# The reversed read of the exponential bias table: from GpSimd's DMA queue to SP's, behind the store it reads

## The reference, cut to what matters

```python
rel = kloc[None, :] - qloc[:, None]                          # (BLOCK, 3*BLOCK)
bias = rel_bias[t5_bucket(rel)].astype(jnp.float32)          # (BLOCK, 3*BLOCK, H)
valid = (jnp.abs(rel) <= WINDOW)[None] & (kpos >= 0) & (kpos < S)
s = jnp.einsum('bnqhgd,bnkhd->bnhgqk', qb, kb) * scale + bias
s = jnp.where(valid[None, :, None, None], s, NEG_INF)
p = jax.nn.softmax(jnp.concatenate([s, sink_col], axis=-1), axis=-1)[..., :-1]
o = jnp.einsum('bnhgqk,bnkhd->bnqhgd', p.astype(v.dtype), vb)
```

## Time and profile before

| | |
|---|---|
| median of 3 runs | 972.08 us (971.94 to 972.39) |
| the profiled execution's own time | 972.42 us |
| its span, slowest core (core 3) | 971.4 us |
| spans of the eight cores | 966.9 to 971.4 us |
| PE busy | 937.4 us, 97% of the span |
| DVE, ACT, POOL busy | 65%, 45%, 27% |
| granted TensorE clock, mean | 0.994 on core 3 |

### The profile page before, as it was taken

One profiled execution on the slowest core, in us unless ns is written; L12 is line 12 of the kernel. 1 busy time (PEld: TensorE's weight loads), 2 busy tenths in 40 slices (PEclk: granted clock), 3 DMA queues, 4 the chain that ended last, 5 costly groups with the idle time before them and its releaser, 6 DMA issues.

```text
span 971.4 us, 16466 instructions; the slowest of 8 cores (966.9 to 971.4 us)
## 1 busy us (share of the span) xinstructions
PE 937.4 (97%) x5501; PEld 437.3 (45%) x5501; DVE 631.5 (65%) x1049; ACT 437.5 (45%) x720; POOL 260.2 (27%) x281
## 2 busy tenths in 40 slices
PE   3999999999999999999999999999999999999996
PEld 1454544553445444444445444444444444444442
DVE  1313476665777757565669798886565666664887
ACT  1125657575663444444457456655110444443111
POOL 3200000111135335343333245543200133333002
PEclk9999999998999999999999999999999999999999
DMA  9998134482439999710668176675533323220312
GB/s 132 163 176 160 24 76 102 64 151 51 66 65 127 119 142 129 103 65 2 131 205 337 31 158 170 165 175 129 173 130 112 111 90 114 85 93 7 131 65 87
DMA packets 39683, 112.12 MB, mean 115 GB/s; under 512 B 4976, under 2 KB 16888, under 8 KB 38608
## 3 DMA queue, kind: packets, MB, share of 16 engines
q0 software_dynamic: 11104, 41.16, 29.2%
q1 hardware_dynamic: 28496, 69.91, 22.7%
HBM read 132.49 MB, written 30.47 MB: 168 GB/s over the span
## 4 chain that ended last, share of the span: by engine, by line
PE 88%; DMA 4%; ACT 3%; DVE 2%; issue 2%; POOL 0%; DVEq 0%; ACTq 0%; POOLq 0%; SPq 0%
PE ps L238 87%; DMA arena<-w_q 2%; DMA arena<-xt 1%; ACT arena L604 1%; DMA gexp_scratch<-arena 1%; PE ps L1283 1%; ACT arena L652 1%; DVE arena L597 0%; ACT arena L607 0%; PE ps L767 0%; PE ps L695 0%; POOL arena L152 0%; ACT arena L731 0%; ACT arena L1521 0%; DVE arena L826 0%
## 5 line engine op out<-in xcount | busy, mean ns | idle before, releaser
L238 PE MATMUL ps<-arena 128*128 128x512 bf16 (+5 forms) x5091 | 921.2, 359 | 23.3 <-DMA arena<-xt 14.6
L238 PEld LDWEIGHTS ps<-arena 128*128 128x128 bf16 (+2 forms) x5091 | 417.2, 98 | 510.1 <-issue 66.8
L1332 ACT COPY arena<-ps 128x512 f32<-128x512 f32 x132 | 76.5, 587 | 132.0 <-PE ps L238 132.0
L1342 POOL TENSOR_TENSOR arena<-arena 128x512 bf16<-128x512 f32 x66 | 89.6, 1358 | 142.0 <-DVE arena L1335 141.9
L1335 DVE TENSOR_TENSOR arena<-arena,ps 128x512 f32<-128x512 f32 x132 | 88.0, 684 | 39.8 <-PE ps L238 39.6
L947 POOL TENSOR_TENSOR arena<-arena 128x512 f32<-128x512 f32 (+1 forms) x48 | 63.8, 1337 | 104.3 <-DVE arena L938 104.1
L1198 ACT ACTIVATE arena<-arena 128x1024 bf16<-128x1024 f32 x26 | 27.5, 1058 | 93.6 <-DVE arena L1647 87.5
L938 DVE SCALAR_TENSOR_TENSOR arena<-arena,ps 128x512 f32<-128x512 f32 x72 | 49.2, 683 | 23.9 <-ACT arena L934 17.1
L1212 POOL TENSOR_TENSOR rs<-mvt,eps_t 128x1 f32<-128x1 f32 x32 | 25.9, 809 | 132.6 <-DVE mvt L1208 90.6
L930 DVE TENSOR_TENSOR arena<-arena,ps 128x512 f32<-128x512 f32 x54 | 37.0, 686 | 35.3 <-ACT arena L927 19.7
L927 ACT COPY arena<-ps 128x512 f32<-128x512 f32 x54 | 31.6, 586 | 55.9 <-PE ps L238 55.9
(11 more groups left out here) (120 smaller groups left out, 577.9 us busy)
## 6 DMA issues: line engine op xcount, KB each, us to landing
arena<-w_bf_cache SPq DMA_DIRECT2D x44, 512.0 KB, 4.2
arena<-u_scratch SPq DMA_DIRECT2D x64, 135.0 KB, 3.7
arena<-x SPq DMA_DIRECT2D x16, 512.0 KB, 13.3
y_scratch<-arena SPq DMA_DIRECT2D x16, 512.0 KB, 7.0
arena<-y_scratch SPq DMA_DIRECT2D x16, 512.0 KB, 5.1
out<-arena SPq DMA_DIRECT2D x15, 512.0 KB, 2.6
arena<-w_f POOLq DMA_DIRECT2D x22, 256.0 KB, 4.8
arena<-w_g POOLq DMA_DIRECT2D x9, 512.0 KB, 19.3
```

The costliest lines, as they stand in the source:

```text
L238: return pe.run(lambda: nc.tensor.matmul(out, lhsT, rhs, start=start, stop=stop, skip_group_check=onto), deps, inc)
L1332: return act.run(lambda: nc.scalar.copy(buf, ps[:, b, :]), deps)
L1342: return pool.run(lambda: nc.gpsimd.tensor_tensor(out=dst, in0=up, in1=gate, op=ALU.mult), deps)
```

## The change

The read of the table back from DRAM gets `sp` as its engine. It then stands in SP's stream right behind the store it waits for, and no longer in POOL's stream ahead of `w_q`. Nothing is computed otherwise, and all transfers have the same shapes.

```diff
         btab["st"] = load(gexp_d.ap(), geb, [t_b1], sp)
-        btab["rev"] = load(Brev, bass.AP(gexp_d, 0, [[1, 128], [512, 8], [1, 384]]), [btab["st"]])
+        btab["rev"] = load(Brev, bass.AP(gexp_d, 0, [[1, 128], [512, 8], [1, 384]]), [btab["st"]], sp)
```

## The result

The changed kernel takes 988.46 us in the median against 972.01 us; the ratio is 1.0169, with a 95% interval from 1.0156 to 1.0182. It is slower by about 16.4 us. That median counts a fourth run, of 1032.94 us, in which the cores of one half of the chip ran at a lower clock; the other three took 987.92 to 988.65 us, and all ratios and the times of the experiments leave such runs out. The loss is there on every core: the spans of the profiled execution go from 981.0 to 987.2 us, 13.6 to 18.3 us more than before, core by core.

A forecast was written before the change was run, and what follows sets the result against it. TensorE, busy 97% of the span, was taken as the bound. 972.4 us plus 13.4 for PE's late restart (the 1.6 gain swallowed within it) plus 3.4 of clock made 989.2, forecast as 989; range 978 to 994.

The forecast's parts named there:

- When the read starts: SP's queue: read issued at about 32.2 us after the store, first packets 3.2 us later, at 35.4.
- How many packets, and how fast: SP's queue: 1040 packets, one per run, alternating with q0's, take 38.9 us; the table lands at 75.8 us.
- Where PE stops: Fourth query group of block 1: PE stands 15 us from about 62.8, going on 13.4 us late at 77.8.
- The clock: PE after its stop: restarts at the lower of two clock levels, losing 3.4 us.
- the two sources of the 3.4: Clock loss: 3.6 us from matmuls after the idle start, 3.0 from another lower-level spell; 3.4 taken between.
- The gain for `w_q`: POOL's queue: `w_q` lands by about 42 or 43 us, ending PE's 1.59 us wait; gain 1.6 us.
- hidden-table rival: SP's queue: table in larger packets, some 190, lands near 44 us, hidden; only 1.6 us gained, 970.8 us; chance 0.13.
- the quicker turn: SP's queue: one packet a run but more than its turn, landing at 61 to 71 us; 972 to 983; chance 0.08.
- the window loads came in time: Rival: window loads 20 us later than forecast make PE wait again before the first convolution; 995 us; chance 0.05.
- my 98: SP's queue behind the table: product stores land by 89 us and window loads by 98, at 216 packets a microsecond.

The follow-up runs named there:

- Experiments 2: Changed kernel with the table still on SP's queue, read as 128 runs of 6144 bytes (other values) instead of 1024 of 768: 972.4 us, ratio 0.9996.
- experiment 4: Changed kernel, but POOL waits for the table before issuing the loads behind `w_q`: 972.2 us, ratio 0.9993.
- Experiments 5: Changed kernel with the three copies moved behind block 1's value projection in DVE's stream: 980.74, 980.92 and 982.30 us, ratio 1.0086.
- experiment 6: Kernel before, with the table's read on POOL's queue moved behind `w_q`, `w_kv`, `w_qm` and `memt`: 973.4 us, ratio 1.0000.
- experiment 3: Kernel before, with the table's read on POOL's queue moved behind both parts of `w_mkv`: 989.2 us, ratio 1.0167.
- experiments 1: Kernel before, with the table's read on POOL's queue moved right behind `w_q`: 972.2 us, ratio 0.9992.

## Why the prediction was right, step by step

**The time.** 989 was forecast, 988.46 measured, and by the chain that was described. That it came out within a microsecond is partly luck: several terms are off by 1 to 3 us and cancel in part, and core 3, for which the sum was made, rose by 15.4 us and not by 16.8.

**When the read starts.** The store landed at 34.20 on core 3, not 31.81: it took 8.36 us instead of 7.62, and had been issued 1.65 us later. SP's first packets came later too: in 34 to 38 us all 119 packets of that core were q0's.

```profile
q0 software_dynamic: 119, 0.70, 100.9%
```

The table's first packet is at 38.17, 2.8 us after my 35.4.

**How many packets, and how fast.** 1040 to the packet. From 36 to 74 us the queues moved 1117 against 1053. The table's own packets run from 38.17 to 75.91, 37.7 us where 38.9 was forecast (37.6 to 38.8 on the eight cores), and it landed 1.1 us behind the last, at 77.0 on core 3 instead of 75.8. The near agreement hides two differences: in that time SP's queue moved 1123 packets, 29.8 a microsecond where 26.7 were forecast, but from 72.2 on 83 of them belonged to the store behind the table. On the eight cores the copies started between 72.9 and 77.1. Experiments 2 and 4 show both factors of this step: fewer packets, or hardly a neighbour, and the table lands by 51 or by 46 on all cores.

**Where PE stops.** At the fourth query group of block 1, for the cast behind the copies: 12.2 us on core 3, 11.5 to 14.4 on the eight. I had 15.0, counted from PE at 62.8. PE came to that group only at 66.74 in this execution: it had begun 0.35 us later, had waited 2.07 us for the inputs of block 1, and had then worked some 3.4 us at the lower clock (0.54 and 0.61 in the halves of 30 to 34 us), so that 188 matmuls took 37.30 us, against 35.62 on four other cores. As the end of the stop is set by the table, this doesn't change the time at which PE goes on: 78.95, 14.6 us after 64.36, where 13.4 was forecast. Experiments 5 and 6 show that it is this place in the streams which sets the price, and 3 that only the time of landing counts.

**The clock.** 5.1 + 0.8 us at half speed cost 2.9 us on core 3, not 3.4; on the eight cores the lower level lasts for 3.0 to 6.0 us of work, which is 1.5 to 3.0 us lost. One of the two sources of the 3.4 is not settled: for the idle start the profile's rows show the full clock (1.00 in 12 to 22 us), and only the matmuls' 0.44 us speak for the lower level. From its restart to the end core 3 needs 907.9 us against 907.0 before (986.8 − 78.95, 971.4 − 64.36), only 0.8 more. Another thing makes up for most of the 2.9: the lower-level spell of the earlier trace rows does not occur on this core in the execution after, which is worth about 3. That is luck of this core: two of the eight cores have such a spell near 225 us before (3 and 4), five have one near 240 us after (0, 4, 5, 6 and 7). Why, no run shows.

**The gain for `w_q`.** This is the one term that the runs do not bear out. In the changed kernel `w_q` landed at 44.4 us (15.19 + 29.2), a little after the 42 to 43 of the forecast and well ahead of PE. PE's wait for it was gone there and in experiments 1, 2 and 4. The ratios of these three are 0.9992, 0.9996 and 0.9993, a gain of 0.4 to 0.8 us, with 1 inside every interval. The hidden-table rival, with 1.6 us, would be 0.9984: at the lower edge of two of the intervals and outside the third. The step took the wait of one core for the gain of the program. Before, three of eight cores wait for `w_q` (0.9, 1.6 and 1.8 us); four of the other five wait 0.9 to 1.9 us for the inputs of block 1 instead, and the slowest core sets the time. With the weights ahead those waits for inputs stand as they were or longer (2.6 us on one core in experiment 2, 3.7 in two waits on one in experiment 4). On two cores of experiment 4 such a wait goes with a spell at the lower clock (0.50 in 31.2 to 34.5 us on core 3), and the 388 matmuls behind it take 64.40 and 64.22 us, against 62.71 on four others. Whether loads queued behind the inputs slow them, or executions just differ, stays open. The sum of 989 did not use this gain; only the hidden-table rival's time did.

**The rivals.** The table in larger packets did not happen on SP's queue, the quicker turn neither, and the window loads came in time: SP's queue was done soon after 92 us, ahead of my 98, with 1785 of its packets in the 8 us from 84 to 92, and the first convolution was emptied at 119.91. The page of the Trainium skill "DMA: Bandwidth & Descriptors", section "Queues, rings and completion order", is borne out in the turns and not in the 9 to 17 descriptors to a packet, as far as SP's queue goes: 1024 runs made 1024 packets, as the trace counts them. On POOL's queue the same runs went about six to a packet (1024 in 176, the 192 less 16 completions).

## What to carry to other kernels

Count the packets of a transfer on the queue that will carry it, and look at whose turns they alternate with: beside a full queue of long packets this read in short runs took about its number of runs times the neighbour's packet time (1024 runs in 37.7 us, beside a neighbour that moved 29.8 packets a microsecond), and an eighth of the runs for the same bytes took a third of the time. A table of many short runs went better in the queue that packs them, placed after what is wanted earlier and before what is wanted later, or in long runs (which here read other values, so the table would have to be laid out for them). No variant was faster than the kernel before beyond its interval. And price a late transfer at the instruction that waits for it: what stands behind it on that engine, and how many buffers its consumers still have, gave 8 us of cover here.

## What the runs showed of the hardware that was not expected

- A short stop cost as much clock as a long one. On core 5 of experiment 5 a stop of 4.03 us was followed by about 5 us of work at the lower clock, on core 3 of the changed kernel one of 12.21 us by 5.9 us. On the eight cores it is 3.4 to 5.5 us of work after stops of 3.3 to 8.3 us, and 3.0 to 6.0 us after stops of 11.5 to 14.4 us. On the two cores named the granted clock had already fallen within the stop (0.70 in 78 to 80 us, and 0.69 in the mean of 12.40 us). On core 2 of experiment 5 it fell only when PE was at work again, from 78.52: 1.00 in 78.0 to 79.5 us, 0.50 in 79.7 to 83.0.
- The first packet came late on SP's queue beside a full q0: issued at 34.26, the table had its first packet at 38.17, and all 119 packets of 34 to 38 us were q0's. On the eight cores it came 3.5 to 4.4 us after the issue. With long runs as well (experiment 2, core 6) the table took 14.4 us for some 10 us of data.
- Holding back all loads behind `w_q` until 46.53 us (experiment 4) left no wait of PE for any of them before 90 us, on any core: they have more slack than their place at the head of a full queue suggests.
